# Two SwiGLU feed-forward layers of a hybrid encoder step: plain tiled products before, one level of Strassen products after

## The chip, the cores and the metric

The kernel runs on one core of a Trainium2 chip. The metric is the device time of one execution in microseconds, as the median of several. All tensors are float32. TensorE (PE) multiplies, VectorE (DVE) and ScalarE (ACT) work elementwise, GpSimd (POOL) adds squares for the norms, and SyncE (SP) issues nearly all DMA transfers, in program order.

## The reference, cut to what matters

One layer of a streaming encoder on 1024 prompt tokens and 8 x 16 sample tokens, 1152 in all, model width 1024, hidden width 2816:

```python
h = x + 0.5 * g1 * swiglu1(modulate(rms(x)))
h = h + gm * mixer(modulate(rms(h)))
h = h + 0.5 * g2 * swiglu2(modulate(rms(h)))
y = modulate(rms(h))

def _swiglu(x, w_gate, w_up, w_down):
    return (jax.nn.silu(x @ w_gate) * (x @ w_up)) @ w_down
```

The shifts, scales and gates of the modulations are 11 vectors of 1024, one set for the prompt and one for each sample (adaLN): silu(c) times a weight matrix of 1024 x 1024 each.

## The kernel before

Everything is kept with features on the partitions: x is [128, 8, 1152]. Each product is made of three matmuls on float32 split into a high part (rounded to the matmul's type by ACT) and a low part (the difference, by DVE): high x high, high x low, low x high (product, lines 333 to 337). Weights come in units of 128 x 1024 through two raw buffers and a ring of six split slots (split_hi, line 319; split_lo, line 324).

A feed-forward layer (ffn on PE, line 1497) is 11 groups of 256 hidden features. A group multiplies two gate and two up units with all 1152 tokens, in three chunks of 384 (column_job, line 1490), makes silu(gate) x up in halves (lines 742, 1118), splits it (lines 744, 1121), and multiplies it with two down units into 24 results, which DVE adds at once to x in SBUF (add_gated, line 1071). So a group has 432 matmuls of 384 columns, 288 of them for gate and up.

The adaLN vectors are made beside it. Three come before the first layer, in halves, with float32 matmuls (line 1448); the other eight one in each of the first eight groups of layer 1: 8 pieces of 512 KB in one buffer, each loaded by SP (line 456), split by ACT and DVE (lines 734, 1095) and used by PE (piece, line 1509) between the group's tiles; fold_half (line 1523) turns the result.

The order of work is fixed by hand: every engine runs its own list of instructions and waits on semaphores that other engines count up. SP loads a group's units one group ahead (ffn_units, line 432) and the pieces between them. The mixer between the two layers (V tiles, eight rounds of mix, the out projection) and the norms follow the same manner; squares are made by ACT, added by POOL, summed across partitions by PE (line 1469), and DVE takes the reciprocals (line 1023) and normalises.

## Time and profile before

| | us |
|---|---|
| runs | 2690.29, 2694.67, 2694.49 |
| median | 2694.49 |
| span of the profiled execution, first to last instruction | 2683.9 |
| the profiled execution's own time | not recorded apart from its span; span and median differ by 10.6 |
| PE busy / DVE busy / ACT busy in that span | 2572.2 / 1337.9 / 807.1 |
| one group of layer 2 | 74.87 |
| one group of layer 1 with an adaLN vector | 85.35 |

PE's busy time joins overlapping matmuls, so how far apart they start tells more than how long each one is. Layer 1 runs from about 88 to 1014 us, the V tiles to about 1131, the rounds of mix and the out projection to 1797, layer 2 to 2642, and the final norm and the stores to the end.

### The profile page before, as it was taken

Reading aid. Unit: us, or ns where it says so; the run is one execution under the profiler, and the core shown is the slowest. Engines: PE = TensorE matmul, PEld = TensorE weight load, DVE = VectorE, ACT = ScalarE, POOL = GpSimd, SP = SyncE. Lnnn points to the kernel's source line nnn. Section 1 sums busy time; section 2 is a strip of 40 time slices with the busy share of each in tenths; the row PEclk is TensorE's granted clock in tenths of the full one; section 3 lists DMA queues with packets and bytes.
Section 4 is the critical chain, followed back from the end, with each engine's and each line's share of the span. In section 5 each row is a group of like instructions: output and inputs, shape, how many; then the busy total and the mean of one; then the engine's idle time right before and its main releaser. Section 6 shows DMA issues by size and latency. Waiting matters only on the chain.

```text
span 2683.9 us, 37363 instructions
## 1 busy us (share of the span) xinstructions
PE 2572.2 (96%) x14394; PEld 2461.3 (92%) x14394; DVE 1337.9 (50%) x2244; ACT 807.1 (30%) x1177; POOL 150.4 (6%) x128
## 2 busy tenths in 40 slices
PE   8699999999999998999999999888999999999996
PEld 3599999999999996799999999788999999999995
DVE  4644344543444437676666666455344434433337
ACT  3622322222221126333343333244111111111115
POOL 3000000000000012011111110020000000000003
PEclk9899999999999999999999999999999999999998
DMA  9132223321221013232222223310111111111101
GB/s 317 55 102 86 73 75 94 102 86 54 93 86 48 31 48 119 89 98 59 59 59 59 59 59 100 120 47 21 42 47 47 37 42 47 47 31 47 31 16 73
DMA packets 196648, 188.21 MB, mean 70 GB/s; under 512 B 8433, under 2 KB 160169, under 8 KB 196342
## 3 DMA queue, kind: packets, MB, share of 16 engines
q1 hardware_dynamic: 194142, 186.79, 22.3%
q10 hardware_dynamic: 2456, 0.75, 0.1%
q8 instruction: 32, 0.52, 0.1%
q14 instruction: 18, 0.15, 0.0%
HBM read 166.99 MB, written 20.53 MB: 70 GB/s over the span
## 4 chain that ended last, share of the span: by engine, by line
PE 83%; DVE 7%; DMA 4%; ACT 4%; issue 2%; SPq 1%; POOL 0%; POOLq 0%; ACTq 0%; DVEq 0%
PE bank L335 26%; PE bank L337 26%; PE bank L336 26%; DMA ada_raw<-in_w_ada 2%; DVE ada_lo L1095 1%; ACT ada_hi L734 1%; PE bank L1509 1%; PE bank L1448 1%; DVE silu L1037 1%; DMA ada_raw<-in_w_ada_final 1%; ACT hfull L677 1%; ACT xn_hi L680 1%; DMA w_ada_sb<-in_w_ada 1%; DVE xn_lo L1041 0%; SPq L397 0%
## 5 line engine op out<-in xcount | busy, mean ns | idle before, releaser
L335 PE MATMUL bank<-xn_hi,w_hi 128*128 128x384 f32 x3264 | 1098.8, 337 | 44.6 <-DVE xn_lo L1041 27.6
L336 PE MATMUL bank<-xn_lo,w_hi 128*128 128x384 f32 x3264 | 1094.3, 335 | 0.0
L337 PE MATMUL bank<-xn_hi,w_lo 128*128 128x384 f32 x3264 | 1094.1, 335 | 0.0
L335 PEld LDWEIGHTS bank<-xn_hi,w_hi 128*128 128x128 f32 x3264 | 615.6, 189 | 55.3 <-issue 42.5
L336 PEld LDWEIGHTS bank<-xn_lo,w_hi 128*128 128x128 f32 x3264 | 615.5, 189 | 1.4 <-issue 0.3
L337 PEld LDWEIGHTS bank<-xn_hi,w_lo 128*128 128x128 f32 x3264 | 615.3, 189 | 0.0
L1118 DVE SCALAR_TENSOR_TENSOR hfull<-silu,bank 128x384 f32<-128x384 f32 x132 | 73.1, 554 | 727.6 <-PE bank L337 725.6
L335 PE MATMUL bank<-h_hi,w_hi 128*128 128x384 f32 x1056 | 355.3, 336 | 0.0
L337 PE MATMUL bank<-h_hi,w_lo 128*128 128x384 f32 x1056 | 353.3, 335 | 0.0
L336 PE MATMUL bank<-h_lo,w_hi 128*128 128x384 f32 x1056 | 353.1, 334 | 0.0
L319 ACT ACTIVATE w_hi<-raw 128x1024 fp32r<-128x1024 f32 x196 | 200.1, 1052 | 389.7 <-PE bank L337 327.2
L324 DVE TENSOR_TENSOR w_lo<-raw,w_hi 128x1024 fp32r<-128x1024 f32 x196 | 237.8, 1243 | 143.8 <-ACT w_hi L319 143.8
L1071 DVE SCALAR_TENSOR_TENSOR x<-bank,ada,x 128x384 f32<-128x384 f32 x368 | 212.8, 612 | 108.9 <-PE bank L337 105.6
L744 ACT ACTIVATE h_hi<-hfull 128x384 fp32r<-128x384 f32 x132 | 69.3, 525 | 542.6 <-DVE hfull L1118 542.6
L335 PEld LDWEIGHTS bank<-h_hi,w_hi 128*128 128x128 f32 x1056 | 198.2, 188 | 5.3 <-DVE x L1079 0.2
L336 PEld LDWEIGHTS bank<-h_lo,w_hi 128*128 128x128 f32 x1056 | 198.2, 188 | 1.8
L337 PEld LDWEIGHTS bank<-h_hi,w_lo 128*128 128x128 f32 x1056 | 198.2, 188 | 0.0
L374 POOL TENSOR_TENSOR acc<-acc,sq 128x384 f32<-128x384 f32 x84 | 89.3, 1063 | 1917.5 <-ACT sq L663 1909.4
L742 ACT ACTIVATE silu<-bank 128x384 f32<-128x384 f32 x132 | 64.9, 492 | 299.2 <-PE bank L337 299.1
L1095 DVE TENSOR_TENSOR ada_lo<-ada_raw,ada_hi 128x1024 fp32r<-128x1024 f32 x64 | 78.4, 1224 | 69.7 <-ACT ada_hi L734 69.7
L1121 DVE TENSOR_TENSOR h_lo<-hfull,h_hi 128x384 fp32r<-128x384 f32 x132 | 73.7, 559 | 78.1 <-ACT h_hi L744 78.1
L734 ACT ACTIVATE ada_hi<-ada_raw 128x1024 fp32r<-128x1024 f32 x64 | 67.4, 1053 | 93.9 <-DMA ada_raw<-in_w_ada 68.5
(166 smaller groups left out, 1908.9 us busy)
## 6 DMA issues: line engine op xcount, KB each, us to landing
ada_raw<-in_w_ada SPq DMA_DIRECT2D x48, 512.0 KB, 3.5
raw<-in_w_in SPq DMA_DIRECT2D x48, 512.0 KB, 4.6
raw<-in_w_ffn_gate SPq DMA_DIRECT2D x44, 512.0 KB, 3.9
raw<-in_w_ffn_up SPq DMA_DIRECT2D x44, 512.0 KB, 5.3
raw<-in_w_ffn_down SPq DMA_DIRECT2D x44, 512.0 KB, 4.4
w_ada_sb<-in_w_ada SPq DMA_DIRECT2D x6, 2048.0 KB, 17.1
ada_raw<-in_w_ada_final SPq DMA_DIRECT2D x16, 512.0 KB, 3.6
x_dram<-x SPq DMA_DIRECT2D x1, 4608.0 KB, 14.2
```

The costliest lines, as they stand in the source:

```text
L319: nc.scalar.activation(w_hi[:, slot, :], raw[:, par, :], ACT.Copy).then_inc(w_hi_ready, 1)
L324: nc.vector.tensor_tensor(w_lo[:, slot, :], raw[:, par, :], w_hi[:, slot, :].bitcast(F32), ALU.subtract).then_inc(w_lo_ready, 1)
L335: nc.tensor.matmul(out, hi, mov_hi, start=first, stop=False, skip_group_check=True)
L336: nc.tensor.matmul(out, hi, mov_lo, start=False, stop=False, skip_group_check=True)
L337: return nc.tensor.matmul(out, lo, mov_hi, start=False, stop=last, skip_group_check=True)
L374: nc.gpsimd.tensor_tensor(acc[:, c, :], acc[:, c, :], sq[:, pos % 3, :], ALU.add).then_inc(acc_added, 1)
L734: nc.scalar.activation(ada_hi[:, :], ada_raw[:, :], ACT.Copy).then_inc(piece_hi_ready, 1)
L744: nc.scalar.activation(h_hi[:, f, c * CH:(c + 1) * CH], hfull[:, q % 2, :], ACT.Copy)\
L1071: nc.vector.scalar_tensor_tensor(x[:, o, cols], ps[:, 0:CH], prompt_scalar(v, o), x[:, o, cols], ALU.mult, ALU.add).then_inc(x_written, 1)
L1095: nc.vector.tensor_tensor(ada_lo[:, :], ada_raw[:, :], ada_hi[:, :].bitcast(F32), ALU.subtract).then_inc(piece_lo_ready, 1)
L1118: nc.vector.scalar_tensor_tensor(hfull[:, q % 2, :], silu[:, q % 2, :], 0.5, bank[3 + c][:, 0:CH], ALU.mult, ALU.mult).then_inc(h_full, 1)
L1121: nc.vector.tensor_tensor(h_lo[:, f, cols], hfull[:, q % 2, :], h_hi[:, f, cols].bitcast(F32), ALU.subtract)\
```

## The change

Both feed-forward layers are computed by one level of Strassen's scheme in Winograd's form: 7 block products in place of 8, over halves of the 512 prompt tokens, halves of the contracted features and pairs of output blocks. The 128 sample tokens are multiplied without it, as stationary operands with 256 moving weight columns. For this

- the normalised input is made once into 7 operands (B11, T1, T2, B21, T3, T4, B22) of 4 x 512, split, and kept in SBUF (ops); the residual x goes to DRAM (x_dram) meanwhile;
- a first pass of 11 rounds makes gate and up: 16 weight tiles a round (8 as loaded, 8 sums or differences of them by DVE), each split; 14 products of 12 matmuls with 512 columns. The four hidden blocks become 7 operands for the second pass, which are split (stage) through three buffers and stored to DRAM (h_dram);
- a second pass of 8 rounds multiplies them with the down weights: four groups of 2, 3, 3 and 3 hidden blocks, two halves of the output each, operands loaded back into eight slots, results added to the residual (x2) in 14 updates a round;
- ahead of a layer's first round DVE and ACT split the first operand (first_operand), the first 8 weight tiles (first_units) and, inside the round, the other operands, all made in x;
- a round's tiles follow each other on PE as A11 with B11 (event P1), sample rows (K0), S1 with T1 (P5), S2 with T2 (P6), A12 with B21 (P2), sample rows (K1), S3 with T3 (P7), A22 with T4 (P4), S4 with B22 (P3), each for two output blocks;
- ACT copies banks whose partial sums are needed twice (snap), DVE adds them (join, update);
- two adaLN vectors instead of three are made ahead, nine in rounds 1 to 9 of layer 1, as 16 pieces of 256 KB in two buffers;
- norms work on 512 prompt columns at a time with the samples apart.

The mixer is changed in places of buffers and waits only. The diff cut to its core (SP, ACT, DVE, PE in this order):

```diff
-GROUPS = NF // 2
+PH = SEQ // 2
+ROUNDS = NF // 2
-FIRST = 3
+FIRST = 2
 LATER = 11 - FIRST
...
+O_B11, O_T1, O_T2, O_B21, O_T3, O_T4, O_B22 = range(7)
+E_P1, E_K0, E_P5, E_P6, E_P2, E_K1, E_P7, E_P4, E_P3 = ((i, i + 1) for i in range(1, 19, 2))
+EVENTS = 18
+WRING = 8
...
+XB, ZB, WB = (0, 3), (1, 4), (2, 5)
+SAMPLE_BANK, ADA_BANK = 6, 7
+GROUPS = ((0, 2), (2, 3), (5, 3), (8, 3))
+SLOTS = ("ABCDEFH", "ABCDGEF", "HABCDGE", "FABCDGE")
...
+    h_dram = nc.dram_tensor("h_dram", [ROUNDS * 7 * P, 2, PH], F32).ap()
...
+            def piece(g, r, first, w, c0):
+                half, k = divmod(r, KT)
+                src = w.rearrange("(k p) n -> p k n", p=P)[:, k, ds((g - first) * D + (c0 + half * HALF), HALF)]
+                if r >= 2:
+                    sp.wait_ge(ada_mm, g * PIECES + (2 * FIRST - PIECES + r - 1))
+                elif not isinstance(g, int) or g > 1:
+                    sp.wait_ge(ada_mm, g * PIECES + (2 * FIRST - PIECES + r - 1))
+                sp.dma_start(ada_raw[r % 2][:, :], src).then_inc(piece_loaded[r % 2], 16)
+            def store_stage(f, g, i):
+                order = (O_B11, O_B22, O_B21, O_T1, O_T3, O_T2, O_T4)[i]
+                s = i % 3
+                sp.wait_ge(stage_lo_ready, of_round(f, g, 7, i + 1))
+                dst = h_dram[ds(g * (7 * P) + order * P, P), :, :]
+                sp.dma_start(dst[:, 0, :], stage_hi[s][:, :].bitcast(F32)).then_inc(stage_stored[s], 16)
+                sp.dma_start(dst[:, 1, :], stage_lo[s][:, :].bitcast(F32)).then_inc(stage_stored[s], 16)
...
+                def round_(g, ada_from=None):
+                    if ada_from is not None:
+                        for r in range(5):
+                            piece(g, r + 2, *ada_from)
+                    next_weights(f, g, 0, 0)
+                    next_weights(f, g, 1, 0)
+                    if ada_from is not None:
+                        for r in range(5, 8):
+                            piece(g, r + 2, *ada_from)
+                    next_weights(f, g, 0, 1)
+                    next_weights(f, g, 1, 1)
+                    if ada_from is not None:
+                        for r in range(8, 11):
+                            piece(g, r + 2, *ada_from)
+                    store_stage(f, g, 0)
+                    if ada_from is not None:
+                        for r in range(11, 14):
+                            piece(g, r + 2, *ada_from)
+                    store_stage(f, g, 1)
+                    store_samples(f, g)
+                    store_stage(f, g, 2)
+                def stores_after(f_, g):
+                    for i in range(3, 7):
+                        store_stage(f_, g, i)
+                def starts(g, ada_from):
+                    for r in range(2):
+                        piece(g, r, *ada_from)
...
+                    with sp.Fori(1, 10 - FIRST) as g:
+                        starts(g, (1, w_ada, FIRST * D))
+                        round_(g, (1, w_ada, FIRST * D))
+                        stores_after(f, g)
...
+                def after(event, rho=-1):
+                    sp.wait_ge(ffn_mm, done(f, ROUNDS + rho, event))
+                after(E_P6[1])
+                load_slot(f, 0, 0)
+                sp.dma_start(x2[:, 0:KH, :], x_dram[:, 0:KH, :]).then_inc(x2_loaded, 16)
...
+                after(E_P4[1])
+                load_slot(f, 0, 3)
+                load_slot(f, 0, 4)
+                store_stage(f, g, 2)
+                after(E_P3[1])
+                load_slot(f, 0, 5)
+                sp.dma_start(x2[:, KH:KT, :], x_dram[:, KH:KT, :]).then_inc(x2_loaded, 16)
+                stores_after(f, g)
+                count = f * ROUNDS + ROUNDS
+                for s in range(3):
+                    sp.wait_ge(stage_stored[s], 32 * count * (3 if s == 0 else 2))
+                sp.wait_ge(hs_stored, 32 * count)
+                load_slot(f, 0, 6)
+                load_samples(1)
+                load_samples(2)
...
+                def stage(g, i, ready, count, src):
+                    act.wait_ge(ready, of_round(f, g, 4, count))
+                    before = i // 3
+                    per = 3 if i % 3 == 0 else 2
+                    if f > 0 or not isinstance(g, int) or g > 0 or before > 0:
+                        act.wait_ge(stage_stored[i % 3], (g * per + (f * ROUNDS * per + before)) * 32)
+                    nc.scalar.activation(stage_hi[i % 3][:, :], src[:, :], ACT.Copy).then_inc(stage_hi_ready, 1)
+                def begin(g):
+                    if not no_round_before(f, g) and (not isinstance(g, int) or g > 0):
+                        act.wait_ge(stage_lo_ready, of_round(f, g - 1, 7, 4))
+                    snap_up(g, 0, E_P1[0], g11[:, :], bank[XB[0]][:, :])
...
+                    stage(g, 3, h_sum, 1, g11)
+                    stage(g, 4, h_sum, 2, g22)
+                    stage(g, 5, h_sum, 3, g12)
+                    stage(g, 6, h_sum, 4, g21)
...
+                    if rho == 0:
+                        count = f * ROUNDS + ROUNDS
+                        for s in range(3):
+                            act.wait_ge(stage_stored[s], 32 * count * (3 if s == 0 else 2))
+                        act.wait_ge(hs_stored, 32 * count)
+                    snap_down(0, 0, E_P1[0], 3)
...
+                def second(g, ada_piece=False):
+                    piece, vector_half = piece_of(g, ada_piece)
+                    weight_sum(dve, f, g + 1, 1)
+                    weight_sum(dve, f, g + 1, 2)
+                    hidden(g, 1, 2, h11, h11, g11)
+                    stage(g, 0, h11)
+                    piece(11)
...
+                    join(g, 5, E_P3[1], h12, bank[ZB[1]])
+                    unit_lo(dve, f, g + 1, 7)
+                    hidden(g, 4, 6, h12, h12, g12)
+                    dve.wait_ge(h_ready, of_round(f, g, 4, 4))
+                    nc.vector.tensor_tensor(g11[:, :], h12[:, :], h11[:, :], ALU.subtract).then_inc(h_sum, 1)
+                    nc.vector.tensor_tensor(g22[:, :], h22[:, :], h12[:, :], ALU.subtract).then_inc(h_sum, 1)
+                    dve.wait_ge(h_sum, of_round(f, g, 4, 1))
+                    nc.vector.tensor_tensor(g12[:, :], h22[:, :], g11[:, :], ALU.subtract).then_inc(h_sum, 1)
+                    dve.wait_ge(h_sum, of_round(f, g, 4, 3))
+                    nc.vector.tensor_tensor(g21[:, :], h21[:, :], g12[:, :], ALU.subtract).then_inc(h_sum, 1)
+                    stage(g, 3, g11)
+                    stage(g, 4, g22)
+                    stage(g, 5, g12)
+                    stage(g, 6, g21)
+                    vector_half(1)
...
+                def prompt(g, u, o, out, first, last_, staged=False):
+                    units_ready(g, u)
...
+                            pe.wait_ge(op_lo_ready, 28 * f + 4 * place + k + 1)
+                        last = product(pe, out[:, :], u_hi[:, u % WRING, k * P:(k + 1) * P],
+                                       u_lo[:, u % WRING, k * P:(k + 1) * P], ops[:, o, 0, k, :], ops[:, o, 1, k, :],
+                                       first and k == 0, last_ and k == KH - 1)
...
+                        pe.wait_ge(gate_act, of_round(f, g - 1, 4, 3))
+                    prompt(g, A11[0], O_B11, X[0], True, False, staged)
+                    piece(0)
+                    if not fresh:
+                        pe.wait_ge(h_ready, of_round(f, g - 1, 4, 3))
+                    prompt(g, A11[1], O_B11, X[1], True, False)
...
+                    samples_in(g, 0, 0)
+                    piece(2)
+                    samples_in(g, 0, 1)
+                    piece(3)
...
+                    prompt(g, A12[0], O_B21, W[0], True, True, staged)
+                    piece(8)
+                    prompt(g, A12[1], O_B21, W[1], True, True)
+                    piece(9)
+                    samples_in(g, 1, 0)
+                    piece(10)
+                    samples_in(g, 1, 1)
+                    piece(11)
...
+                    pe.wait_ge(joined, of_round(f, g, 6, 3))
+                    prompt(g, S4[0], O_B22, Z[0], False, True, staged)
+                    pe.wait_ge(joined, of_round(f, g, 6, 4))
+                    prompt(g, S4[1], O_B22, Z[1], False, True)
+                    fold_half(1)
...
+                round_(0, staged=True)
+                if f == 0:
+                    with pe.Fori(1, LATER + 1) as g:
+                        round_(g, True)
+                else:
+                    with pe.Fori(1, ROUNDS - 1) as g:
+                        round_(g)
+                round_(ROUNDS - 1)
+                for rho in range(DOWN):
+                    down(rho)
```

## Rows read from the trace of the kernel before

**Rows 1.** Busy time of each engine, its share of the span and its instructions.
```profile
PE 2572.2 (96%) x14394; PEld 2461.3 (92%) x14394; DVE 1337.9 (50%) x2244; ACT 807.1 (30%) x1177; POOL 150.4 (6%) x128
```

**Rows 2.** The chain that ended last, shares of the span by engine.
```profile
PE 83%; DVE 7%; DMA 4%; ACT 4%; issue 2%; SPq 1%; POOL 0%; POOLq 0%; ACTq 0%; DVEq 0%
```

**Rows 3.** Timeline of SP: start us, us, engine, line, operation.
```profile
1894.17 0.38 SPq L397 DMA_DIRECT2D raw<-in_w_ffn_gate  x1
...
1969.05 0.38 SPq L397 DMA_DIRECT2D raw<-in_w_ffn_gate  x1
```

**Rows 4.** Timeline of PE: first and last matmul of runs of 384, 512, 256 columns.
```profile
1900.06 0.33 PE L337 MATMUL bank<-xn_hi,w_lo 128*128 128x384 f32 x1
...
1906.64 0.33 PE L336 MATMUL bank<-xn_lo,w_hi 128*128 128x384 f32 x1
...
1059.77 0.39 PE L335 MATMUL bank<-w_hi,xn_hi 128*128 128x512 f32 x1
...
1067.93 0.39 PE L335 MATMUL bank<-w_hi,xn_hi 128*128 128x512 f32 x1
...
1185.40 0.28 PE L1661 MATMUL bank<-ws_parts,s_hi 128*128 x1
...
1187.41 0.28 PE L1662 MATMUL bank<-ws_parts,s_lo 128*128 x1
```

**Rows 5.** Windows: us, busy us of each engine, granted clock, DMA share, GB/s.
```profile
155.18:240.53 85.35, 85.03 (x482) 80.04 (x481) 39.06 (x69) 23.81 (x30) 0.00 (x0) 1.00 0.29 86
1799.00:1804.00 5.00, 0.00 (x0) 0.00 (x0) 4.23 (x9) 3.78 (x7) 2.01 (x2) 0.65 0.00 2
1804.00:1809.00 5.00, 4.95 (x18) 4.35 (x19) 5.00 (x4) 1.04 (x2) 0.00 (x0) 0.66 0.41 119
41.00:75.00 34.00, 32.80 (x86) 7.70 (x87) 8.77 (x10) 6.17 (x10) 1.07 (x2) 0.95 0.66 232
```

**Rows 6.** The chain in order of time, in one adaLN group: start us, us, what.
```profile
156.57 3.57 DMA ada_raw<-in_w_ada
160.17 1.07 ACT ada_hi L734
161.26 1.24 DVE ada_lo L1095
```

**Rows 7.** Waits of PE: us in total, times, longest.
```profile
PE bank L1509 <- DVE ada_lo L1095: 5.9, 10, 1.2
```

**Rows 8.** Groups by line and shape: busy us, mean ns, idle before.
```profile
L324 DVE TENSOR_TENSOR w_lo<-raw,w_hi 128x1024 fp32r<-128x1024 f32 x196 | 237.8, 1243 | 143.8 <-ACT w_hi L319 143.8
...
L1121 DVE TENSOR_TENSOR h_lo<-hfull,h_hi 128x384 fp32r<-128x384 f32 x132 | 73.7, 559 | 78.1 <-ACT h_hi L744 78.1
...
L1071 DVE SCALAR_TENSOR_TENSOR x<-bank,ada,x 128x384 f32<-128x384 f32 x368 | 212.8, 612 | 108.9 <-PE bank L337 105.6 <-DVE h_lo L1121 2.8
...
L826 ACT ACTIVATE v_all<-bank 128x512 f32<-128x512 f32 x18 | 10.2, 600 | 43.6 <-PE bank L337 43.6
...
L1023 DVE RECIPROCAL acc<-acc 128x384 f32<-128x384 f32 x12 | 30.6, 2548 | 8.5 <-ACT acc L667 8.4
```

**Rows 9.** Timeline of DVE, two splits in a row.
```profile
1804.38 2.29 DVE L324 TENSOR_TENSOR w_lo<-raw,w_hi 128x1024 fp32r<-128x1024 f32 x2
```

**Rows 10.** DMA issues: count, KB each, median us to landing.
```profile
x_dram<-x SPq DMA_DIRECT2D x1, 4608.0 KB, 14.2
...
merged_dram<-merged SPq DMA_DIRECT2D x7, 576.0 KB, 3.6
```

**Rows 11.** Timeline of PE: an adaLN half, three places where stages end.
```profile
30.78 7.04 PE L1448 MATMUL bank<-w_ada_sb,cT 128*9 128x512 f32 x16 [0.26 <-DMA w_ada_sb<-in_w_ada]
...
1804.05 1.65 PE L1469 MATMUL bank<-acc,ones 128*128 128x384 f32 x2 [7.38 <-POOL acc L374]
...
1025.10 1.65 PE L1469 MATMUL bank<-acc,ones 128*128 128x384 f32 x2 [11.00 <-POOL acc L374]
...
2641.36 0.34 PE L337 MATMUL bank<-h_hi,w_lo 128*128 128x384 f32 x1
```

2009 lines of the change are left out of this document (1385 added, 624 removed).

## Prediction

> **What bounds the kernel now.** I read the engine totals first [rows 1]: TensorE (PE) works 96% of the 2683.9 us span, VectorE (DVE) 50%. The chain of waits [rows 2] says the same: 83% of what ended last is PE. Then the feed-forward groups. In the second layer a group takes 74.87 us from one gate-weight issue to the next [rows 3], and its 432 matmuls of 384 columns at one pitch fill that exactly. 38 steps of the same line from 1900.06 to 1906.64 give 173.3 ns [rows 4]. So 11 plain groups are 823.6 us of uninterrupted PE, and a layer ends when its columns have been streamed. In the first layer eight groups also compute an adaLN vector each, in 8 pieces; such a group takes 85.35 us and PE is busy for 85.03 [rows 5]. The chain there runs load, ScalarE (ACT) copy, DVE subtraction, again and again [rows 6], yet PE waited for a piece 5.9 us in all [rows 7]: the round trips are hidden, because pieces lie 8 to 16 us apart. The profiled execution's span is 2683.9 us and the median of the runs 2694.5, so 10.6 us lie around it; I add them at the end. This kernel's measurement can tell about 0.2% from no change.
>
> **What the change takes away: columns.** Pitches by width [rows 4]: 384 columns 173.3 ns, 512 columns 226.7 ns (36 steps in 8.16 us), 256 columns 118 ns (17 steps in 2.01 us), that is 2.4 GHz plus some 13 ns for each matmul. A first-pass round has 14 tiles x 12 = 168 matmuls of 512 columns and 48 of 256 for the sample rows: 38.1 + 5.7 = 43.8 us. A second-pass round with n=3 has 126 and 36: 28.6 + 4.2 = 32.8; with n=2 84 and 24: 21.9. A layer is 11 x 43.8 + 6 x 32.8 + 2 x 21.9 = 722 us against 823.6: **101 us less, 202 for both**.
> The Trainium skill (TensorE: Matmul & The Clock Gate, "Wait — 56ns, not 53.3ns?") puts the fixed part of a warm matmul at about 2.5 ns. By it a layer would go from 772 to 685 us, 88 less, and my total would end 27 us higher; the trace's 13 ns disagree, and the trace decides.
>
> **Prices of what is added.** DVE: 1024 elements 1243 ns, 384 elements 559 ns [rows 8], so 512 take 0.70 us behind a wait; two of 1024 in a row take 2.29 us [rows 9], 0.1 less each, so 0.61 us for one of 512 that follows without a wait. With a bank and the gate as operands 384 elements take 612, so 512 take 0.75. ACT: 600 ns for 512 out of a bank [rows 8], 0.63 from SBUF. DMA: 576 KB land in 3.6 us and 4608 KB in 14.2 [rows 10], a line that gives 2.7 us for 256 KB, 2.1 for none and 380 GB/s between; over its whole time the large one moves 332 GB/s. An issue costs SP 0.38 us [rows 3].
>
> **Plain rounds.** DVE has 45 operations of 512 (16 low parts, 8 weight sums, 6 joins, 4 products, 4 sums, 7 stagings), about 31 us, ACT 33, about 21, both inside 43.8. Stage buffer 0 serves stagings 0, 3 and 6, so staging 6 waits until 3 has landed: 10 us into the next round; then ACT copies bank X, which PE wants at 13.6. It fits, 3 us to spare: 44.1 us a round. Cover gone, each microsecond later counts.
>
> **Rounds with an adaLN vector: the stall.** There are nine now (FIRST goes from 3 to 2), with 16 pieces each of 256 KB in two buffers. PE works 43.8 + 32 x 0.23 for the pieces + 1.4 for folds and turns = 52.6 us. But SP issues pieces 0 and 1 of a round only behind stores_after of the round before, and PE runs piece(0) already after its first tile. I count from the end of the last tile (S4, second half): DVE join 0.70, low part 0.61, product 0.70, four sums 2.6, staging 3 0.6 and its wait: 5.5. Its store: 0.4 issue, 2.7, hops 0.3: 8.9. ACT 0.63, DVE 0.70: staging 6 ready at 10.2. SP issues its two stores (0.8), turns its loop, issues piece 0, which moves behind those 512 KB: 14.5 landed. ACT and DVE: 15.9. PE got there at 3.3 (fold 0.6, tile 2.7) and **waits 12.6 us**. Such a gap also drops the granted clock: after 7.38 us of waiting [rows 11], 1799 to 1804 shows a granted clock of 0.65 and 1804 to 1809 0.66, with 18 matmuls where 28 would fit [rows 5]: 2 us more.
> Then the round trip: matmul of piece r, SP 0.15, 2.7, ACT 0.63, DVE 0.70, 4.3 us until piece r+2 can run. Two tiles take 5.4, so mostly hidden; between pieces 1 and 3 lie only sample rows of 1.4 us (0.5 lost, the half clock hides the rest). Piece 7 is issued behind the next weights, which wait for unit 13's low part, and behind their 512 KB: 2 us. Piece 10 comes behind the next weights again (1.4), and piece 11's subtraction stands on DVE behind join, two weight sums, product and staging 0 (3.0). Together 52.6 + 12.6 + 2 + 0.5 + 2 + 4.4 = **74 us a round**. Bounds: with a load at the 2.1 us that none would take and the later stalls gone, 63; with each 512 operation at its 0.70 and each piece behind 512 KB of other traffic, 82. I take 74, since each hop has its own row.
>
> **First round.** The transformed operands are made in x, by DVE, first. PE's adaLN halves: 7.0 us each [rows 11]; the third now waits for 1 MB more of weights ahead of it, 3 us, and two halves go; the fourth ends near 60. Behind it on DVE: 14 operations of first_units (9), B11, and then about 70 operations until B22's low parts (49, with waits): P7 can start near 121, and the round ends at **139 us**, with DVE 3 us behind it.
>
> **Second pass.** ACT's first copy there waits until all stages of the last round are stored. Ahead of staging 3's store SP has issued slots D, E, F and half of x2, 5.5 MB, 17 us at 332 GB/s from 5.5 us before the round's end: it lands at 14.8, staging 6 at 20. PE wants the copy at 7.2: **13.5 us, and 2 for the clock, in each layer**. In n=2 rounds DVE has 24 x 0.42 + 14 x 0.75 = 20.6 us against 21.9, and PE's next tile waits for the update of X: 1.7 us twice. In n=3 rounds 24 us against 32.8: hidden. Slots: 12.6 MB in 38 us at 332 GB/s; the last is wanted 48 us after the first can be issued: hidden. A pass is 240.6 + 15.5 + 3.4 = 259 us.
>
> **Sum, layer 1.** 139 + 3 + 9 x 74 + 48.3 (round 10, which waits 4.5 for the last vector) + 259 = 1115, against PE's last matmul at 1014.1 (it waited 11.00 until 1025.10 [rows 11]): +101. **V tiles**: two reciprocals of 512 (one of 384 takes 2548 ns [rows 8]) and the row-by-row normalising let the first tile run 12 us: +5. **Layer 2**: from the out projection's end at 1796.7 (1804.05 less 7.38 [rows 11]): reciprocals, first operand, first_units 30 us, round 0 another 60, 10 x 44.1, 259 = 790, against 845 to 2641.7 [rows 11]: -55. **Tail**: -3. 2683.9 + 101 + 5 - 55 - 3 = 2732, and with 10.6: **2743 us, 1.8% slower**. The 202 us of columns are given back in layer 1: 9 x 21.4 = 193 us of stalls where there were 8 x 1 us.
>
> **Rivals.**
> 1. Faster: the pieces' round trips hide better. For: in the kernel before they cost PE 5.9 us in all. Against: there SP issued them behind nothing that depends on the last matmul of the round. At 63 us a round: 2743 - 9 x 11 = 2644. It turns faster below 68.6 us a round (48 us over nine). 24%.
> 2. Slower still: plain rounds lose their 3 us of slack as well (a stage store landing at 4 us instead of 2.7 moves PE's wait, twice in the chain); 3 to 5 us in 19 rounds: 2800 to 2838. For: 576 KB stored take 3.6 us [rows 10]. Against: 256 KB should not. 13%.
> 3. DRAM cannot feed the second pass: at the 232 GB/s of 41 to 75 us [rows 5] the first transition is 8 us later, the n=2 to n=3 one 6, in both layers: 2771. For: nothing before moved 230 GB/s for long beside PE. Against: 4.6 MB at 332. 10%.
> 4. No change: the stalls come out at 69 us a round. 3%.
> My forecast 50%. Range: from rival 1's end to rival 2's start, with first round and passes uncertain by 10 us each: 2660 to 2830. Faster 0.24, within 0.2% 0.03, slower 0.73.
>
> **What would show it.** In the profile after: 512-column matmuls 226 ns apart; in the first 900 us TensorE at 6 or 7 tenths and dips of granted clock at a spacing of 74 us, with PE waits on ada_lo of 12 us, nine times; the chain of waits there through ada_raw loads, h_dram stores, ACT and DVE; plain rounds 44 us apart in layer 2 with PE at 9; one gap of 13 us before the second pass, released by ACT's snap. I am wrong if adaLN rounds lie under 68 us apart, or if PE waits on DVE in plain rounds.

## The result, and the profile after

The changed kernel takes **2805.8 us** (median of 4 runs, 2802.8 to 2808.8) against 2694.3 for the kernel before beside it: a ratio of **1.042**, 95% interval 1.0406 to 1.0435. I forecast 2743, range 2660 to 2830, slower with 0.73. The side was right and the range held the time, but the loss is 111 us where I gave 49, 2.3 times as much: the size was wrong. Beside the experiments the kernel before had medians of 2692.9 to 2693.1.

Of the page of the changed kernel: engine totals, PE's busy tenths, the granted clock and the DMA rate in 40 slices, and the chain's shares.

```profile
PE 2446.6 (87%) x12152; PEld 2087.3 (74%) x12152; DVE 1712.1 (61%) x2651; ACT 1072.2 (38%) x1834; POOL 132.8 (5%) x95
...
PE   7677777777787899699999999989699999979996
...
PEclk9789999999998999999999999999799999989998
...
GB/s 311 38 139 135 139 130 139 130 135 139 138 122 276 253 214 180 105 78 129 57 56 56 56 56 58 85 133 81 47 120 147 135 131 152 117 305 238 214 180 70
...
PE 69%; DVE 11%; DMA 9%; issue 5%; ACT 3%; SPq 1%; POOL 1%; DVEq 0%; ACTq 0%; POOLq 0%
```

PE was busy 96% and is busy 87% of a longer span [rows 1]; its part of the chain fell from 83% to 69% [rows 2], and the difference went to DVE, DMA and "issue". The PE line shows where: sixes and sevens through the first eleven slices (the first round and the adaLN rounds), a seven in slice 13 (where the first layer's second pass starts), a six in slice 29 (the second layer's first round), nines in its plain rounds, a seven in slice 36 (its second pass starts). The waits of PE (total, times, longest, us):

```profile
PE bank L2410 <- DVE ada_lo L1728: 171.9, 45, 13.1
PE bank L447 <- issue: 50.7, 7, 16.6
PE bank L447 <- ACT g L1131: 18.8, 4, 4.7
PE bank L2335 <- POOL acc L976: 15.9, 5, 8.3
...
PE bank L447 <- DVE x L1888: 9.6, 5, 2.7
```

The wait for pieces of adaLN weights was 5.9 us [rows 7] and is 171.9.

**The columns** came out as forecast. The timeline of PE in the second layer (start us, us):

```profile
2052.64 0.39 PE L448 MATMUL bank<-ops,u_hi 128*128 128x512 f32 x1
...
2054.68 0.39 PE L448 MATMUL bank<-ops,u_hi 128*128 128x512 f32 x1
```

Nine steps in 2.04 us, 227 ns each. The windows of an adaLN round, of a plain round and of three rounds of the second pass (us, busy us of PE, PEld, DVE, ACT, POOL, granted clock, DMA share, GB/s):

```profile
376.70:451.80 75.10, 56.70 (x267) 43.58 (x267) 39.93 (x65) 29.40 (x53) 0.00 (x0) 0.91 0.43 136
...
2097.44:2141.61 44.17, 44.17 (x219) 37.47 (x219) 29.43 (x48) 19.01 (x36) 0.00 (x0) 1.00 0.40 137
883.50:925.80 42.30, 25.21 (x109) 19.59 (x107) 19.48 (x39) 11.19 (x26) 0.00 (x0) 0.80 0.76 279
925.80:955.80 30.00, 24.47 (x108) 19.53 (x108) 19.40 (x38) 10.35 (x22) 0.00 (x0) 0.94 0.76 276
...
993.30:1026.20 32.90, 32.90 (x163) 27.93 (x163) 21.84 (x39) 11.33 (x22) 0.00 (x0) 1.00 0.67 249
```

A plain round is 44.17 us with PE busy throughout; adaLN rounds are 75 us with 56.7 busy; the first two rounds of the second pass (42.3, 30.0) hold 21.9 us of matmuls each; its fourth round runs without a gap at 32.9, and the four after it take 32.9 to 33.8.

**The stall that cost most** is seen in the chain of one adaLN round, whose last tile ended at 376.7 (start us, us, what):

```profile
381.22 0.69 DVE stage_lo L1711
...
382.60 2.18 DMA h_dram<-stage_lo
384.80 0.64 ACT stage_hi L1139
385.46 0.70 DVE stage_lo L1711
...
387.82 2.78 DMA ada_raw<-in_w_ada
...
390.71 0.64 ACT ada_hi L1148
391.37 0.70 DVE ada_lo L1728
...
392.20 0.61 PE bank L2410
```

Counted from 376.7: staging 3 ready 5.2 (I had 5.5), staging 6 ready 9.5 (10.2), piece 0 issued at 11 and landed at 13.9 (14.5), its low part at 15.4 (15.9), and PE waited 11.62 us (12.6).

Stage by stage, from the times at which PE ends its tiles:

| stage | forecast, us | measured, us | difference |
|---|---|---|---|
| round 0 of layer 1 ends | 139 | 148.6 | +9.6 |
| then to the end of 9 adaLN rounds | 3 + 9 x 74 = 669 | 684.7 | +15.7 |
| round 10 | 48.3 | 50.2 | +1.9 |
| second pass, layer 1 | 259 | 275.4 | +16.4 |
| V tiles, against before | +5 | +18.9 | +13.9 |
| mixer and out projection, against before | 0 | -0.8 | -0.8 |
| round 0 of layer 2 | 90 | 93.6 | +3.6 |
| ten plain rounds | 441 | 441.7 | +0.7 |
| second pass, layer 2 | 259 | 270.1 | +11.1 |
| tail, against before | -3 | -0.2 | +2.8 |

The differences sum to 75, as do the spans: 2807.0 against my 2732. The 10.6 us that I added for what lies around the span is not there: runs of either kernel take 1.8 us more than their own span. By that the profiled execution of before, with its span of 2683.9 us, took about 2685.7, some 9 us less than that kernel's median (this is an estimate; its own time is not recorded). So against the median the miss is 63.

### The profile page after: what moved, and what is told of

It reads as the page before. It is cut to its first block, busy times and chain, and to the rows that moved or that the text cites. A ratio compares the mean times of both kernels' runs of the same rounds, so it can differ in the third digit from the quotient of the medians.

```text
span 2807.0 us, 36682 instructions
## 1 busy us (share of the span) xinstructions
PE 2446.6 (87%) x12152; PEld 2087.3 (74%) x12152; DVE 1712.1 (61%) x2651; ACT 1072.2 (38%) x1834; POOL 132.8 (5%) x95
## 4 chain that ended last, share of the span: by engine, by line
PE 69%; DVE 11%; DMA 9%; issue 5%; ACT 3%; SPq 1%; POOL 1%; DVEq 0%; ACTq 0%; POOLq 0%
PE bank L447 20%; PE bank L448 20%; PE bank L449 20%; DMA ada_raw<-in_w_ada 4%; DVE u_lo L524 1%; PE bank L2391 1%; PE bank L2389 1%; PE bank L2387 1%; DMA ada_raw<-in_w_ada_final 1%; DMA wraw<-in_w_ffn_down 1%; POOL acc L976 1%; PE bank L2410 1%; ACT ada_hi L1148 1%; DVE ada_lo L1728 1%; PE bank L2412 1%
## 5 line engine op out<-in xcount | busy, mean ns | idle before, releaser
L447 PE MATMUL bank<-ops,u_hi 128*128 128x512 f32 x1232 | 499.4, 405 | 46.7 <-ACT g L1131 18.8
L448 PE MATMUL bank<-ops,u_hi 128*128 128x512 f32 x1232 | 494.3, 401 | 0.0
L449 PE MATMUL bank<-ops,u_lo 128*128 128x512 f32 x1232 | 491.4, 399 | 0.0
L524 DVE TENSOR_TENSOR u_lo<-wraw,u_hi 128x512 fp32r<-128x512 f32 (+2 forms) x532 | 316.8, 617 | 229.0 <-ACT u_hi L518 226.8
L447 PE MATMUL bank<-xn_hi,w_hi 128*128 128x384 f32 x1152 | 388.3, 337 | 15.7 <-DVE xn_lo L2230 9.7
L448 PE MATMUL bank<-xn_lo,w_hi 128*128 128x384 f32 x1152 | 386.1, 335 | 0.0
L449 PE MATMUL bank<-xn_hi,w_lo 128*128 128x384 f32 x1152 | 386.0, 335 | 0.0
L447 PEld LDWEIGHTS bank<-ops,u_hi 128*128 128x128 f32 x1232 | 240.6, 195 | 110.7 <-issue 31.8
L449 PEld LDWEIGHTS bank<-ops,u_lo 128*128 128x128 f32 x1232 | 239.4, 194 | 52.9
L448 PEld LDWEIGHTS bank<-ops,u_hi 128*128 128x128 f32 x1232 | 240.2, 195 | 50.0
L447 PEld LDWEIGHTS bank<-xn_hi,w_hi 128*128 128x128 f32 x1152 | 217.1, 188 | 21.4 <-issue 13.7
L448 PEld LDWEIGHTS bank<-xn_lo,w_hi 128*128 128x128 f32 x1152 | 217.1, 188 | 0.2 <-issue 0.2
L449 PEld LDWEIGHTS bank<-xn_hi,w_lo 128*128 128x128 f32 x1152 | 217.1, 188 | 0.0
L2410 PE MATMUL bank<-ada_hi,c_parts 128*18 128x512 f32 x144 | 59.1, 410 | 171.9 <-DVE ada_lo L1728 171.9
L1148 ACT ACTIVATE ada_hi<-ada_raw 128x512 fp32r<-128x512 f32 x144 | 90.5, 629 | 283.5 <-DMA ada_raw<-in_w_ada 215.3
L2410 PEld LDWEIGHTS bank<-ada_hi,c_parts 128*18 128x18 f32 x144 | 13.9, 97 | 188.5 <-issue 112.2
```

What stands on the lines that cost most here:

```text
L447: nc.tensor.matmul(out, hi, mov_hi, start=first, stop=False, skip_group_check=True)
L448: nc.tensor.matmul(out, hi, mov_lo, start=False, stop=False, skip_group_check=True)
L449: return nc.tensor.matmul(out, lo, mov_hi, start=False, stop=last, skip_group_check=True)
L524: nc.vector.tensor_tensor(unit(u_lo, u, n), unit_source(u, n), unit(u_hi, u, n).bitcast(F32), ALU.subtract).then_inc(u_lo_ready, 1)
L1148: nc.scalar.activation(ada_hi[r % 2][:, :], ada_raw[r % 2][:, :], ACT.Copy)\
L2410: nc.tensor.matmul(bank[ADA_BANK][0:2 * NSEQ, :], c_parts[:, k, :], ada_hi[r % 2][:, :], start=k == 0, stop=False, skip_group_check=True)
```

## The experiments

Each starts from the changed kernel (1.042) and is given as its ratio to the kernel before, run beside it on the same chip. All compute the same function.

**1. SyncE's order alone.** Pieces 0 and 1 of the next round are issued ahead of the late stores.

```diff
-                    with sp.Fori(1, 10 - FIRST) as g:
-                        starts(g, (1, w_ada, FIRST * D))
-                        round_(g, (1, w_ada, FIRST * D))
+                    starts(1, early)
+                    stores_after(f, 0)
+                    with sp.Fori(1, 9 - FIRST) as g:
+                        round_(g, early)
+                        starts(g + 1, early)
                         stores_after(f, g)
```

> SyncE alone is changed: it issues pieces 0 and 1 of the next adaLN round ahead of the four late stage stores of this one, not behind them; ScalarE and VectorE keep their order (piece 0 behind staging 6). In the changed kernel TensorE waits 11.5 to 13.0 us for piece 0 in each of nine rounds of about 75.2 us. Theory A (my prediction: staging 6 is ready 10.2 us after the round's last tile, then the load is issued and lands 4.3 us later): the load has landed long before, so the wait falls to about 8 us, 4.4 us less in each of nine rounds: 2766 us, rounds of 71 us. Rival B (the wait is set by the staging chain on ScalarE and VectorE alone, the load hardly counts): within 1 us a round, 2797 to 2806. Rival C (the load is all of it): the wait goes to under 3 us, about 2715.

Measured: 2763.2 us, 1.0251 (1.0229 to 1.0272). Rounds are 71.1 us on average from the second on, and the wait at piece 0 fell from about 12 to 6.5. Waits of PE and one round's window:

```profile
PE bank L2414 <- DVE ada_lo L1732: 119.2, 44, 7.9
...
504.70:576.20 71.50, 59.20 (x268) 45.38 (x268) 39.99 (x66) 29.18 (x54) 0.00 (x0) 0.90 0.46 143
```

Theory A (2766) stands, B (2797 or more) and C (2715) fall: SyncE's place of the load was 43 us; that the rest of the wait is the staging chain on ACT and DVE is for the next run to show. One thing is not as drawn. Over the nine rounds PE waits for pieces 52.7 us less than in the changed kernel, but the rounds are only 44.0 us shorter, because PE is busy 521.4 us for 512.8, at a mean granted clock of 0.93 for 0.92. The window is the round in which this shows most (59.2 us busy at 0.90; the same round of the changed kernel has 56.5 at 0.93); three other rounds have 0.95 and 56.2 to 57.2 us. The shorter gap did not bring the clock back.

**2. Pieces 0 and 1 early on all three engines.**

```diff
                     store_stage(f, g, 1)
+                    if next_from is not None:
+                        starts(g + 1, next_from)
                     store_samples(f, g)
...
                     rows_of(1)
+                    for r in range(2):
+                        piece_of(g + 1, ahead)[0](r)
                     act.wait_ge(joined, of_round(f, g, 6, 5))
...
+                    for r in range(2):
+                        piece_of(g + 1, ahead)[0](r)
                     join(g, 5, E_P3[1], h12, bank[ZB[1]])
```

> Pieces 0 and 1 of the next round are moved into the round before on all three engines: SyncE issues them behind the second stage store, ScalarE copies them ahead of the last gate, VectorE subtracts ahead of the last join. Nothing else changes, the arithmetic is the same. Theory A (the round's cost over 44.2 + 8.7 us of PE work is mostly the wait for piece 0 and the clock that falls behind it): the wait of 12 us goes and the clock stays up, 14 us less in each of nine rounds, rounds near 61 us, 2680 us: faster than the kernel before (2694). Rival B (the waits are a latency of the piece loop that only moves: with piece 0 early, pieces 2 and 3 are now waited for): half comes back, rounds near 68 us, 2743. Rival C: the two operations put ahead of the late stagings push stage 6, and with it ScalarE's first bank copy, past TensorE's need: rounds 61 plus 1 to 2 us.

Measured: 2743.3 us, 1.0184 (1.0167 to 1.0201), Rival B's number. Rounds are 68.9 us on average (76.1 in the changed kernel). The wait at piece 0 is gone, and two others came:

```profile
PE bank L2416 <- DVE ada_lo L1733: 89.0, 36, 9.3
...
PE bank L2393 <- DVE ada L1743: 18.9, 8, 2.4
```

The second row is the sample rows' wait for the vector's second half, which DVE finishes behind staging 6; the first holds a new wait of 3.0 to 4.4 us (9.3 in the first of the nine rounds) at piece 2, which SyncE's list still has behind the late stage stores. Half of the 14 us came back: my stall was the first of several behind the same chain.

**3. All sixteen pieces spread evenly.** PE's order; the other engines follow it:

```diff
+                    piece(0)
                     prompt(g, A11[0], O_B11, X[0], True, False, staged)
-                    piece(0)
+                    piece(1)
...
                     samples_in(g, 1, 0)
-                    piece(10)
                     samples_in(g, 1, 1)
-                    piece(11)
+                    piece(10)
...
                     prompt(g, S4[0], O_B22, Z[0], False, True, staged)
+                    piece(15)
```

On DVE (ACT and SyncE alike) pieces 0 to 3 of the next round go among the late stagings, and the vector's second half ahead of them:

```diff
                     hidden(g, 4, 6, h12, h12, g12)
+                    next_piece(1)
+                    vector_half(1)
...
+                    next_piece(2)
                     stage(g, 3, g11)
                     stage(g, 4, g22)
+                    next_piece(3)
                     stage(g, 5, g12)
                     stage(g, 6, g21)
-                    vector_half(1)
```

> The same 16 pieces a round, spread evenly: TensorE takes piece 0 ahead of the round's first tile, one piece behind each later tile or pair of sample groups, piece 15 behind the second last tile; SyncE, ScalarE and VectorE do pieces 0 to 3 of the next round among this round's late stores and stagings, and VectorE finishes the vector's second half ahead of them. No piece stands within 1.4 us of another any more. Theory A (all waits of the adaLN rounds come from where the pieces stand against their round trip of 4.3 us, none from the work itself): a round is its matmuls, 44.2 + 7.3 for 32 piece matmuls + 1.4 for folds and turns = 52.9 us, nine times 23.2 less than the changed kernel's 76.1: 2597 us; with 1 to 2 us of rest a round up to 2615. That is faster than the kernel before (2693). Rival B (the pieces saturate something else: VectorE has 16 subtractions more, about 11 us, on top of its 31 in a round of 53, and its in-order queue holds them up): rounds of 60 to 65, 2660 to 2705. Rival C (the granted clock stays below full speed even without long waits): PE busy but rounds of 57, 2634.

Measured: 2677.2 us, **0.9936** (0.9921 to 0.9951): 0.6% faster than the kernel before. Waits of PE, and one round:

```profile
PE bank L2419 <- DVE ada_lo L1735: 58.4, 57, 2.1
...
466.50:527.70 61.20, 55.16 (x267) 41.83 (x267) 39.76 (x65) 28.93 (x53) 0.00 (x0) 1.00 0.52 163
```

The nine rounds went from 76.1 to 62.4 us on average (the one shown: 61.2) with the same matmuls and splits, which settles that most of the adaLN loss was order. Theory A's 52.9 us is not reached: 58.4 us of short waits remain, 1.0 us each, 6.5 a round, and PE is busy 55.2 us at a granted clock of 1.00, so my count of its work was 2 us short as well. The round time is in Rival B's interval (60 to 65 us). That DVE is saturated is not so: it is busy 39.8 of 61.2 us, and at the pieces that PE waits for its subtraction starts about 0.1 us behind the end of ACT's copy (0.8 at piece 5). Where the remaining waits come from can be read in this trace, though no run tried it. The longest, at piece 15 (1.9 us on average) and piece 12 (1.2), follow loads that SyncE issues 4.4 and 4.0 us after their buffer is free, right behind a stage store in its list; at piece 11 (1.5) ACT starts the copy 3.3 us after the load has landed. It is order again. SyncE in the round shown, at piece 15:

```profile
518.86 0.36 SPq L643 DMA_DIRECT2D h_dram<-stage_lo  x1
519.45 1.00 SPq L634 DMA_DIRECT2D ada_raw<-in_w_ada  x2
```

Rival C is out as a price of 4 us in every round: the granted clock is 1.00 in five of the nine rounds, the one shown among them, and 0.97 in four, where PE is busy 56.2 to 57.0 us.

**4. The order of transfers at the second pass.** In the changed kernel PE waits there for 16.6 us in one piece. SyncE's timeline, the last tile of the first pass having ended at 883.5:

```profile
885.04 0.49 SPq L741 DMA_DIRECT2D x<-x_dram  x1
888.47 0.34 SPq L642 DMA_DIRECT2D h_dram<-stage_hi  x1
...
903.58 0.33 SPq L642 DMA_DIRECT2D h_dram<-stage_hi  x1
...
906.74 1.00 SPq L664 DMA_DIRECT2D hs_in<-hs_dram  x2
910.26 3.67 SPq L613 DMA_DIRECT2D wraw<-in_w_ffn_down  x4
```

Staging 6's store goes out at 903.6, 20.1 us after the tile, where I had staging 6 at 20. The waits of PE do not end with that. The chain ahead of the third round's first tiles, which begins at 955.8:

```profile
940.56 8.58 DMA wraw<-in_w_ffn_down
...
957.76 0.67 DVE x L1888
958.48 0.50 PE bank L447
```

First only the stores were moved, ahead of slots 4 and 5 and of the residual's second half:

```diff
                 load_slot(f, 0, 3)
-                load_slot(f, 0, 4)
                 store_stage(f, g, 2)
                 after(E_P3[1])
-                load_slot(f, 0, 5)
-                sp.dma_start(x2[:, KH:KT, :], x_dram[:, KH:KT, :]).then_inc(x2_loaded, 16)
                 stores_after(f, g)
+                load_slot(f, 0, 4)
+                load_slot(f, 0, 5)
...
                 load_slot(f, 0, 6)
+                sp.dma_start(x2[:, KH:KT, :], x_dram[:, KH:KT, :]).then_inc(x2_loaded, 16)
```

> Only the transition to the second pass is changed, in both layers: the last round's four late stage stores are issued ahead of the loads of operand slots 4 and 5 and of the second half of the residual, which come behind them. In the changed kernel the first matmul that needs ScalarE's first copy waits 16.6 us (883.5 + 7 to 906 us), and the first second-pass round takes 42.2 and 40.9 us where its matmuls are 21.9. Theory A (5.5 MB of loads are issued ahead of the stores, which land behind them at 20 us): the stores land near 13 us, the wait falls to about 6 us, 10 us less in each layer: 2786 us. Rival B (the wait is the stage chain on ScalarE and VectorE, 10.2 us, and the stores are not held up by the loads): 0 to 3 us in all, 2803 to 2806. Rival C: slots 4 and 5 now come too late and the wait moves behind the copy: 2800 to 2810.

Measured: 2800.7 us, 1.0405 (1.0388 to 1.0423), an interval that overlaps the changed kernel's. The passes as a whole, 271.6 and 268.9 us, are not shorter either: where nothing in them was changed they take 271.9 to 275.4 and 268.6 to 274.7. The chain, and a wait of DVE, tell why:

```profile
884.24 7.01 issue
...
904.20 8.57 DMA wraw<-in_w_ffn_down
...
DVE s L551 <- DMA wraw<-in_w_ffn_down: 11.6, 2, 11.3
```

PE's wait for the copy fell to 7.0 us, near Theory A's 6 (6.4 in layer 2), and a new one of 9.1 us (8.4) took its place. The four weight loads of the next round land 8.6 to 16.5 us after their issue, behind the residual's 2304 KB and the sample operands' 1536 KB. DVE stands at their sum for 11.3 us, and behind it stand the updates that the round's last tiles wait for. That is Rival C with another late transfer than the one it named. (The expectation of the next run has 10.4 and 12.7 us for these two waits of PE; the trace shows 7.0 and 9.1.) So in the next run whatever that round does not need went behind those weights:

```diff
                 load_slot(f, 0, 6)
-                load_samples(1)
-                load_samples(2)
...
                             next_weights(f, g, 1, 1)
+                        if rho == 0:
+                            sp.dma_start(x2[:, KH:KT, :], x_dram[:, KH:KT, :]).then_inc(x2_loaded, 16)
+                            load_samples(1)
+                            load_samples(2)
```

> Second pass only: the late stage stores go ahead of slots 4 and 5, and the second half of the residual (2304 KB) and the sample operands of the later groups (768 KB each) go behind round 0's next weights; the second slot of group 1 goes behind the weights of round 1's second half. With the stores alone moved (the run before this one) TensorE's wait for the first copy fell from 16.6 to 10.4 us, but the first second-pass round still took 42 us, because the next weights (8.6 us to land behind the residual) held VectorE's weight sum, and behind it the updates that the last tiles wait for. Theory A (what is issued ahead of these weights on SyncE's queue is what delays them): they land in 4 to 5 us, the wait of 12.7 us before the round's last tiles falls to under 4, and rounds 11 and 12 take 34 and 26 us: 8 to 12 us less in each layer than in the changed kernel, 2784 to 2790. Rival B (DMA bandwidth is the limit, everything lands later by what goes ahead): 2798 to 2804.

Measured: 2779.6 us, 1.0319 (1.0304 to 1.0335). The first two rounds of the pass are 31.5 and 26.9 us in layer 1 (42.3 and 30.0 in the changed kernel) and 30.8 and 25.1 in layer 2; the passes take 261.5 and 258.9 us, well outside what unchanged ones take. Theory A, though the weights still land in 5.6 to 6.9 us and not in 4 to 5; Rival B is out, for nearly the same bytes (11.1 MB for 11.8) now move in three quarters of the time:

```profile
883.30:914.80 31.50, 24.34 (x108) 19.45 (x106) 19.43 (x39) 11.31 (x26) 0.00 (x0) 0.89 0.98 353
```

The DMA engines are busy 0.98 of this stretch, so here the rate may be the next limit; no run tried that.

**5. The weights in a queue of their own.** The same loads with the same waits are issued by ACT, in two places of its round; `down_weights` is new.

```diff
-                        weights_next = rho + 1 < DOWN
+                        weights_next = False
...
                     snap_down(1, 0, E_P6[0], 12)
+                    down_weights(g, 0)
                     unit_hi(act, f, g, 14)
                     snap_down(1, 1, E_P6[1], 14)
                     unit_hi(act, f, g, 15)
+                    down_weights(g, 1)
```

> The weights of the second pass (28 loads a layer) are issued by ScalarE's queue, not by SyncE's behind the operand slots and their waits. In the changed kernel such a load takes 6.9 to 9.0 us from issue to landing beside the slots, and rounds 12 and 13 of each layer take 30.0 and 37.5 us (26.8 and 35.9 in the second) where their matmuls are 21.9 and 32.8. Theory A (the weights come late because they stand in one queue behind 1 MB slots): the loads land in 3 to 4 us and some 3 to 5 us go in each layer: 2797 us. Rival B (DRAM or the 16 DMA engines are the limit there, whichever queue): the same landing times, within 2 us of 2806. Rival C (the gaps there are TensorE waiting for VectorE's updates of the banks, 2.7 us at the start of round 13 in both layers): these stay whatever the queue.

Measured: 2864.9 us, 1.0637 (1.0619 to 1.0654), 59 us **slower** than the changed kernel, which none of my theories allowed. The second passes take 305.3 and 300.6 us (275.4 and 270.1), and in the chain stands

```profile
937.77 22.34 DMA wraw<-in_w_ffn_down
```

for a load of 384 KB. Between 883 and 1110 us such loads take 7.4 us in the median on ACT's queue (20 loads) and 3.6 on SyncE's (24):

```profile
wraw<-in_w_ffn_down ACTq DMA_DIRECT2D x20, 384.0 KB, 7.4
...
wraw<-in_w_ffn_down SPq DMA_DIRECT2D x24, 384.0 KB, 3.6
```

The four loads that stand beside the slots of 1536 KB at this place land 10.3, 14.8, 18.2 and 22.3 us after their issue; in the changed kernel the same four take 3.7, 5.6, 8.8 and 8.6. There SyncE's list has them among the slots, and its waits for their buffers hold the later slots back; now SyncE waits for none of them, and slot C goes out 53.6 us after the last round's end for 57.8. Between 940 and 955 us the two queues (q1 is SyncE's, q10 ACT's; packets, MB, share) moved

```profile
q1 hardware_dynamic: 1181, 4.65, 79.2%
q10 hardware_dynamic: 1223, 1.20, 23.4%
```

about as many packets each, but SyncE's are four times as large, so ACT's queue got a fifth of the bytes. In the changed kernel's one queue these loads and slots land in the order in which they were issued, so a load that is issued ahead of the slots is served ahead of them; on two queues the small one shares with all that the other holds. The Trainium skill (DMA: Bandwidth & Descriptors, "Issuing engines are not separate DMA queues") says that DMAs of several engines run on the same 16 DMA engines and interleave. The trace agrees, and adds the price here: up to 22.3 us for 384 KB.

**6. The third weight load of the V tiles**, ahead of SyncE's waits for the residual rows.

```diff
-                if q == 1:
+                if q == 2:
                     sp.wait_ge(x_written, XW_FFN1)
```

> Between layer 1 and the V tiles: SyncE issues the third weight load of the V tiles (q = 2) ahead of its waits for the residual and sample rows and of their 2 MB of stores, not behind them. In the changed kernel that load lands at 1173.4 us, VectorE stands at its low part until 1175.8 and only then takes the second reciprocal, and TensorE's V tiles run at full pace from 1192.8. Theory A (VectorE's order behind this load sets when the V tiles start): the reciprocal comes 5 to 6 us sooner and all behind it: 2801 us. Rival B (the normalising itself, 16 steps of 0.7 us a half on VectorE, or the ring of weights sets the start): within 1 us of 2806.

Measured: 2801.0 us, 1.0403 (1.0387 to 1.0419). From PE's last tile of layer 1 to V tiles at full pace it is 30.4 us (34.0 in the changed kernel, whose chain is below). By the time of the kernel alone the interval touches the changed kernel's, but the stage tells them apart: from layer 1's last tile to the end of the out projection it is 796.3 to 797.3 us in the three kernels with this edit (this one and the two of experiment 8) and 799.5 to 800.9 in the eight without. Theory A, then, with some 4 us for its 5 to 6.

```profile
1158.88 1.53 POOL acc L976
...
1163.20 3.35 DVE acc L1604
...
1168.44 4.93 DMA raw<-in_w_in
...
1175.84 3.26 DVE acc L1604
```

**7. Round 0.** The chain in the changed kernel holds a wait for DMA ahead of the staging and the copy that PE wants:

```profile
124.74 5.79 DMA wraw<-in_w_ffn_up
...
131.24 0.69 DVE h L1719
...
133.89 0.50 ACT g L1131
```

```diff
                     unit_hi(act, f, 0, 11)
+                    unit_hi(act, f, 0, 12)
+                    unit_hi(act, f, 0, 13)
                     op_hi(f, O_T3)
                     op_hi(f, O_T4)
-                    unit_hi(act, f, 0, 12)
-                    unit_hi(act, f, 0, 13)
...
+                    if not fresh:
+                        weight_sum(dve, f, g + 1, 1)
+                        weight_sum(dve, f, g + 1, 2)
                     hidden(g, 1, 2, h11, h11, g11)
                     stage(g, 0, h11)
+                    if fresh:
+                        weight_sum(dve, f, g + 1, 1)
+                        weight_sum(dve, f, g + 1, 2)
```

(and units 12 and 13 likewise ahead of T4's sums and low parts on DVE)

> Only round 0 of each layer is changed: the parts of units 12 and 13, behind whose low parts the next round's first weights are issued, are made ahead of the last operand's, and VectorE takes the two weight sums for round 1 behind the first product and its staging, not ahead of them. In the changed kernel the last weights of round 1 are issued behind 124.7 us and land at 130.5; VectorE stands at the weight sum, ScalarE at the staging behind it, and TensorE waits 4.7 us (layer 1, to 134.4) and 4.6 us (layer 2, to 2039.1) for a bank copy. Theory A (this wait for a DMA in VectorE's order is what my step for the first round left out): both waits go to under 1 us, 2806 less 8 = 2798 us. Rival B (VectorE's queue of 70 operations is 4 us behind in any case): the waits only move to the later tiles, 2803 to 2807.

Measured: 2796.1 us, 1.0384 (1.0370 to 1.0398). Round 0 of layer 1 ends at 143.5 us for 148.6, and that of layer 2 takes 90.5 us for 93.6 (93.4 to 93.7 in the kernels whose first rounds were not changed): 8.2 us, Theory A's size. The waits before that copy are 1.6 and 1.9 us, not quite under 1, and the one before them grew from 4.7 to 5.9. So in layer 1 only 1.9 us of the gain are waiting; the rest is that PE is busy 3 us less in the round, at a granted clock of 0.87 for 0.83.

**8. Together.** Even pieces, order of the pass, V load:

> The three changes before this one together (even pieces, order in the second pass, the third weight load of the V tiles sooner). If each loss stands by itself, the gains add: 2806 less 209 (even pieces), less 20 (pass), less 5: 2572 us, 4.5% faster than the kernel before. If they share a cause (DMA bandwidth or VectorE's queue), the sum is smaller than the parts: over 2590.

Measured: 2645.0 us, **0.9818** (0.9805 to 0.9831). From the changed kernel that is 161 us less; the parts by themselves were 129, 26 and 5: they add. My 2572 was too low because I had 209 for the even pieces, which gave 129. With round 0 as well:

> The combined kernel (even pieces, order in the second pass, third V weight load sooner: 2645 us) with the changed first rounds as well. If the first rounds' waits stand by themselves: 8 us less, 2637 us; if round 1's waits, larger than those of the later rounds there (66.7 us against 61.6), take some of it, 2633 to 2645.

Measured: 2636.8 us, **0.9783** (0.9770 to 0.9796), the fastest kernel here, 2.2% under the kernel before. Of its page:

```profile
PE 2425.3 (92%) x12152; PEld 2066.4 (78%) x12152; DVE 1711.0 (65%) x2651; ACT 1069.0 (41%) x1834; POOL 132.8 (5%) x95
...
PEclk9799999999999998999999999998899999999998
```

The same number of matmuls as the changed kernel, in 168 us less of span.

## Why the prediction was right on the side, and which steps of it failed

The columns and the stall at piece 0 were right as mechanisms, and they decide the side. The size was not: 111 us lost for 49. The step that failed is in "Second pass": it took the wait for ACT's first copy as the whole loss and called the rest hidden ("Slots: ... hidden"), 259 us a pass, where the runs showed 275.4 and 270.1: most of what was missing lies in the second and third rounds, behind weights that land late on the same queue. The other terms were mis-sized: the nine adaLN rounds by 15.7 us, the V tiles by 13.9, the two first rounds by 13.2, the tail by 2.8; and a term of 10.6 us that does not exist hid part of it.

- **Columns**: right. 226.7 ns a matmul of 512 and rounds of 44.17 (I had 44.1), 32.9 (32.8): the 101 us a layer are there.
- **Plain rounds**: right, with the 3 us of slack; PE never waits in ten of them. Rival 2 is out.
- **adaLN rounds**: the mechanism was right and its hops were right to a microsecond, and experiments 1 to 3 show it by taking it apart. The size was 684.7 us for 669. In the round of the chain above, 75.1 for 74.1, the wait at piece 0 is 11.6 (I had 12.6), the later stalls are 6.8 (1.1, 2.0, 1.3 and 2.4; I had 6.9), and PE is busy 56.7 where I had 52.6 and 2 for the clock. Evenly fed it is busy 55.2 at a granted clock of 1.00, so the count of its work was 2.6 us short (its 1.4 us for folds and turns stands on no row) and the clock costs 1.5. The first, eighth and ninth of the nine rounds take 77.7 to 78.4; why is not traced. Rival 1 was a fair idea of what order can do: its 63 us a round is what even pieces give (62), but it does not come by itself.
- **First round**: mis-sized, 9.6 us in layer 1 and 3.6 in layer 2. Its two tiles for P7 start at 121.8 us, as forecast (121), but from there the round takes 26.8 us for 18. I costed it by DVE's operations ("49, with waits") and left out that the weights of round 1 are issued only behind units 12 to 15, so that DVE's sum, first in its queue for the second half, waits for a DMA of 5.8 us and PE for 4.7. And I put down nothing for the clock: the tile behind each of the two waits of 4.7 us takes 5.0 and 5.1 us, where a tile at full clock takes 2.7. Experiment 7 took back 5.1 of the 9.6.
- **Second pass**: the step that failed. PE's wait for the copy was 16.6 us for 13.5: staging 6's store goes out at 20.1 us, where I let the wait end, and still has to land. But against the forecast the first round of the pass is only 3 us long (42.3 for 39.1); the second is 6 longer (30.0 for 23.6) and the third 5 (37.5 for 32.8), and there I had no wait but the 1.7 us for an update. PE waits 5.6 and 2.7 us in these two, and the granted clock is 0.94 and 0.95. The transfers ahead delay the next weights too, DVE waits for them in order, and bank updates stand behind. The second run of experiment 4 took back 13.9 and 11.2 us a pass, but that is no repair of the miss alone: 10.8 us of it in layer 1 come from the first round, most of which I had priced, 3.1 from the second, and the third stayed at 37.5. Rival 3 gave a like sum (+8 and +6 a layer) for a reason that does not hold: at 279 GB/s the rate was not the limit, since after reordering the same stretch moves 353.
- **V tiles and tail**: mis-sized by 13.9 and 2.8 us. "+5" priced reciprocals and normalising, and left out GpSimd's adds of squares (1.3 us and more each, eleven of them one behind the other from 1142.1 to 1160.4), the weight load behind SyncE's waits (experiment 6: 4 us), and DVE's order of reciprocal, samples, low part, reciprocal. The adds were not tried alone, so their share is argued, not shown.
- **The 10.6 us around the span**: wrong, and by luck it hid 12 us of the miss. By the 1.8 us of all other runs it was not time around the span but mostly a fast execution of the kernel before.

What stays open: the first, eighth and ninth adaLN rounds; why PE is busy longer in experiment 1 with a shorter gap; and the 2.7 us before the third round of a pass, where PE waits for an update of a bank by DVE, which is still 2.7 in the last run of experiment 4.

## What to carry to other kernels

A cut of PE's feed-forward work by 12% was worth +4.2% or -2.2% of the time with the very same instructions: price the order of each in-order queue, each DMA's place in it included, before the columns. When a stall is removed, look for the next piece of work behind the same chain: taking one wait out gave half of it back, spreading all of them gave most of the rest. And in a stretch where DMA is dense, what is issued ahead of a small, urgent load is its latency; here it was better placed first on the busy queue than on another.

## What the runs showed of the hardware

- Of two queues with work, each moved about as many packets (1181 and 1223 in 15 us), so the one with packets of 1 KB got 1.20 MB beside 4.65 MB of the one with packets of 4 KB. A 384 KB load took up to 22.3 us so; the same loads, issued ahead of the 1536 KB ones on one queue, took 3.7 to 8.8.
- PE's granted clock over the nine adaLN rounds, which have the same matmuls in all four kernels:

| kernel | nine rounds, us | PE waits for pieces and vectors, us | PE busy, us | mean granted clock |
|---|---|---|---|---|
| changed (one wait of 12 us a round) | 684.7 | 171.9 | 512.8 | 0.92 |
| experiment 1 (one of 6.5) | 640.7 | 119.2 | 521.4 | 0.93 |
| experiment 2 (3 to 4, and shorter ones) | 620.5 | 107.9 | 512.6 | 0.96 |
| experiment 3 (none over 2.1) | 561.9 | 58.4 | 502.8 | 0.99 |

- Behind the 11.6 us wait of the round shown, matmuls of 512 columns start 0.43 us apart until 396.0 us and 0.23 apart from then on: the lower of the clock's two levels for 3.8 us.
- A run takes 1.8 us more than the span from its first to its last instruction, in both kernels.
